# Cache pages with two consecutive tokens per partition, on even and odd partitions

## What is computed

```python
# sample attention: block-sparse (MoBA), blocks of 256 tokens = 2 pages, best 3 of 8 blocks
page_sum = jnp.sum(cache_k[layer_idx, page_table].astype(jnp.float32), axis=2)
...
kmean = jnp.sum(page_sum.reshape(bsz, nb, pages_per_block, N_HEADS, HEAD_DIM), axis=2) / MOBA_BLOCK
gate = jnp.einsum('bthd,bnhd->bthn', q, kmean)        # chooses the blocks
s = jnp.einsum('bthd,bthnd->bthn', q, k_g) / math.sqrt(HEAD_DIM)
s = s - slopes[None, None, :, None] * dist            # ALiBi: dist = position of q - position of key
p = jax.nn.softmax(jnp.where(valid, s, -jnp.inf), axis=-1)
att = jnp.einsum('bthn,bthnd->bthd', p, v_g)
...
z = x @ w_in                                          # [q | k | v | B | C | h], 1024 x 3072
mix = jnp.concatenate([att, gb * conv_y], axis=-1) @ w_out
x1 = layer_norm(DEEPNORM_ALPHA * x + mix, ln1_g, ln1_b)
up, ffn_buf_new = causal_dwconv(x1 @ w_up, ffn_buf, w_fconv)
f = (jax.nn.silu(a) * g) @ w_down                     # a, g = split(up)
y = layer_norm(DEEPNORM_ALPHA * x1 + f, ln2_g, ln2_b)
```

## Time and profile before

| | |
|---|---|
| three runs | 440.43, 440.23, 439.62 us |
| their median | 440.23 us |
| the profiled execution's own time | 439.81 us |
| span from its first to its last instruction | 438.0 us |
| PE, DVE, ACT, POOL busy | 412.9, 295.2, 181.2, 106.5 us |
| DMA packets, bytes | 109515, 124.86 MB |
| mean TensorE clock granted | 0.991 |

### The profile page before, as it was taken

The page is one execution under the profiler, slowest core; times in us unless marked ns, Lnnn a source line. Parts: engine busy times, 40 slices in busy tenths (PEclk is TensorE's granted clock), DMA queues, the critical chain, the costliest instruction groups (busy, mean ns, idle before and its releaser), DMA issues.

```text
span 438.0 us, 8235 instructions
## 1 busy us (share of the span) xinstructions
PE 412.9 (94%) x2903; PEld 339.1 (77%) x2903; DVE 295.2 (67%) x382; ACT 181.2 (41%) x694; POOL 106.5 (24%) x133
## 2 busy tenths in 40 slices
PE   5999999999999998999999989999999999999990
PEld 5588887876866774765554479999999999999990
DVE  0498999999799976954441274667766776534437
ACT  1587469644378233112110234544455555233201
POOL 1004134995255221100000707122211221000002
PEclk9999999999999999999999999999999999999996
DMA  8999999899999999999999933655566665667002
GB/s 316 393 362 407 405 407 378 323 393 408 410 353 364 354 400 405 405 405 404 404 402 402 353 113 97 193 172 160 162 179 194 196 194 179 190 202 215 2 1 99
DMA packets 109515, 124.86 MB, mean 285 GB/s; under 512 B 5775, under 2 KB 66920, under 8 KB 109466
## 3 DMA queue, kind: packets, MB, share of 16 engines
q1 hardware_dynamic: 101138, 107.56, 69.9%
q10 hardware_dynamic: 8336, 16.78, 10.2%
HBM read 121.90 MB, written 2.61 MB: 284 GB/s over the span
## 4 chain that ended last, share of the span: by engine, by line
PE 57%; DVE 18%; SPq 9%; issue 6%; DMA 5%; POOL 2%; ACT 1%; DVEq 0%; POOLq 0%; ACTq 0%
PE ps L1807 11%; PE ps L1808 11%; PE ps L1809 11%; SPq L352 7%; DVE qk L929 6%; DVE T L939 5%; PE ps L1700 4%; PE ps L1424 4%; PE ps L1619 4%; PE ps L1595 3%; PE ps L1621 3%; PE ps L1371 3%; DMA wring<-in_cache_v 2%; DMA KV<-in_cache_k 2%; POOL x1l L603 1%
## 5 line engine op out<-in xcount | busy, mean ns | idle before, releaser
L1176 DVE TENSOR_TENSOR wlo<-KV,whi 128x2048 fp32r<-128x2048 f32 (+1 forms) x24 | 61.8, 2575 | 57.1 <-ACT whi L829 29.1
L1424 PE MATMUL ps<-xT,wring 128*128 128x264 f32 x384 | 89.6, 388 | 0.1
L1424 PEld LDWEIGHTS ps<-xT,wring 128*128 128x128 f32 x384 | 71.6, 190 | 13.5 <-issue 1.7
L1807 PE MATMUL ps<-x1h,whi 128*128 128x264 f32 x256 | 73.7, 288 | 0.2
L1808 PE MATMUL ps<-x1l,whi 128*128 128x264 f32 x256 | 72.6, 284 | 0.0
L1809 PE MATMUL ps<-x1h,wlo 128*128 128x264 f32 x256 | 72.5, 283 | 0.0
L929 DVE TENSOR_TENSOR qk<-KV,qk 128x1536 f32<-128x1536 f32 (+1 forms) x32 | 67.5, 2111 | 5.7 <-DMA KV<-in_cache_k 2.2
L660 ACT ACTIVATE qk<-qk 128x64 f32<-128x64 f32 x216 | 51.8, 245 | 29.7 <-POOL qk L551 21.6
L939 DVE TENSOR_REDUCE T<-qk 128x24 f32<-128x1536 f32 (+1 forms) x32 | 58.4, 1827 | 0.0
L1807 PE MATMUL ps<-fh,whi 128*128 128x264 f32 x176 | 50.3, 286 | 0.1
L1808 PE MATMUL ps<-fl,whi 128*128 128x264 f32 x176 | 49.9, 284 | 0.0
(11 more groups left out here) (213 smaller groups left out, 572.4 us busy)
## 6 DMA issues: line engine op xcount, KB each, us to landing
KV<-in_cache_k SPq DMA_DIRECT2D x128, 256.0 KB, 6.5
KV<-in_w_ffn_up SPq DMA_DIRECT2D x32, 512.0 KB, 4.7
KV<-in_cache_v SPq DMA_DIRECT2D x60, 256.0 KB, 7.9
wring<-in_cache_v SPq DMA_DIRECT2D x56, 256.0 KB, 6.9
KV<-in_w_ffn_down SPq DMA_DIRECT2D x8, 1408.0 KB, 6.4
wring<-in_w_in ACTq DMA_DIRECT2D x5, 2048.0 KB, 14.1
zbuf<-in_cache_v SPq DMA_DIRECT2D x12, 256.0 KB, 5.2
zbuf<-in_w_ffn_up SPq DMA_DIRECT2D x3, 1024.0 KB, 10.3
```

What stands on the lines that cost most here:

```text
L1176: nc.vector.tensor_tensor(wlo[s][:, 0:n], w2[s][:, 0:n], whi[s][:, 0:n], ALU.subtract).then_inc(s_lo, 1)
L1424: ins = nc.tensor.matmul(ps[:, z_bank(n), 0:R], tile[k], xT[:, k, :], start=k == 0, stop=k == KT - 1)
L1807: nc.tensor.matmul(out, wh[k], xh[k], start=k == 0, stop=False)
```

## The change

`load` keeps its four `dma_start` for a group and their order, but each page now goes to every second partition. Page g of a group lands on the partitions of parity g % 2, and fills there the columns of both pages of its pair (g - g % 2 and the next): token 2i lies in the first of them, token 2i+1 in the second, on partition 2i + g % 2. In HBM the two tokens are 4 KB in a row, and in SBUF the two columns are 4 KB in a row. In the built program each of these DMAs has 64 rows of 1024 floats on either side (a step of two partitions on the SBUF side), where it had 128 rows of 512. There are 256 such DMAs, so their packets fall from 32768 to 16384; the bytes stay.

A block's 512 rows of K (or V) fill the same 128 x 2 places as before in another order, so nothing else changes but the table of distances. No instruction is added, removed or moved on any engine.

```diff
             def load(pages, ids, dst, landed):
                 for g in range(GP):
-                    sp.dma_start(dst[:, g, :], pages[bass.ds(ids[g], 1)].rearrange("o t d -> (o t) d")).then_inc(landed, 16)
+                    sp.dma_start(dst[g % 2:P:2, g - g % 2:g - g % 2 + 2, :],
+                                 pages[bass.ds(ids[g], 1)].rearrange("o (t j) d -> (o t) j d", j=2)).then_inc(landed, 16)
...
     tok = np.arange(P)
-    past = PAST - (np.arange(NPAGE)[None, :] * PAGE + tok[:, None])
+    g = np.arange(NPAGE)[None, :]
+    past = PAST - ((g - g % 2 + tok[:, None] % 2) * PAGE + tok[:, None] // 2 * 2 + g % 2)
```

## The result

The changed kernel takes 449.44 us (median of four runs, 447.76 to 451.94) where the kernel before takes 440.33 (four runs, 439.62 to 441.15). The ratio is 1.0212, with a 95% interval of 1.0171 to 1.0254: slower by 9.1 us. Forecast were 438.5 and a gain as the likeliest sign. The profiled execution took 448.5 us, with a span of 446.7; that of before had 439.81 and 438.0. In the changed kernel all lines behind L352 stand one higher, so L1596 is the `values` of before's L1595.

What follows compares the result with a forecast made beforehand. The V stretch was taken as bounded nearly equally by the page stream and PE's own list. Terms -1.7 + 1.9 - 1.9 = -1.7 gave 438.5 us against the median, own range 436.6 to 440.3, 8-in-10 range 436.6 to 452.

Steps and rivals of the forecast that it cites:

- What costs nothing: SP's page issues, the other engines' work and the clock: no cost; a 64-row issue, 0 to 0.5 us, stays under 0.62.
- rival 1: Page writes to SBUF: even and odd partitions collide, rate under 403 GB/s, price 455 us, ends 441 and 484; chance 0.30.
- Term 1: V stream, 150 to 240 us: 425 GB/s in place of 403 closes PE's gaps on DMA, -1.7 us.
- Term 2: K part: `w_in` gets less beside 4 KB pages, chunk 2 lands late, `z_tile(8)` stalls, +1.9 us (1.1 to 3.7).
- Rival 2: K part: K never runs dry, so `w_in` starves at several chunks, 442.3 us; chance 0.08.
- Term 3: PE's gaps at 67.57 (for ACT) and 100.68 us (for DVE's penalties) swallow the lateness from `z_tile(8)`, -1.9 us.
- Rival 3: Page stream: 4 KB pages run at 403 GB/s too, no faster rate, 440.2 us; chance 0.08.
- The clock: Whole kernel: granted clock was 1.00 in each window; with fewer gaps no cause was seen for another.

Runs made afterwards that it cites:

- spwait4: The kernel before with four already-true waits on SP behind each page load, taking only SP's time: 444.75 us, ratio 1.0109.
- fixed_after: The changed kernel with constant page numbers in place of the page table, so table reads and register instructions are gone: 440.81 us, ratio 1.0020 to the kernel before.
- filled: The changed kernel with four unread matmuls added on PE ahead of two waits in the V part: 448.63 us, ratio 1.0206 to the kernel before.
- pairs_k: The kernel before with the change's load for K pages alone, V pages loaded as before: 445.04 us, ratio 1.0114.
- fixed_before: The kernel before with constant page numbers, so table reads and register instructions are gone: 439.42 us, ratio 0.9981.
- pairs_v: The kernel before with the change's load for V pages alone, K pages loaded as before: 442.97 us, ratio 1.0062.
- spwait6: The kernel before with six already-true waits on SP behind each page load, taking only SP's time: 456.19 us, ratio 1.0329.

## Why the prediction was wrong, step by step

**The step that failed: "What costs nothing".** It bounded the issue of a 64-row load at 0 to 0.5 us and said that "either stays under 0.62". The bound on the issue was right, 0.475. The comparison was wrong: it set the issue alone against the engines' time for a page. Before's own trace had the rest. The issue is 0.33, but SP goes from group to group in 2.07 us, so 0.52 for a page; 0.18 of that are register instructions and the time between instructions. With them, the upper bound was 0.5 + 0.18 = 0.68, above 0.62, and the edit had a price. The page table's 0.97 us for each sample, 0.06 for a page, was left out as well. Measured are 0.67, or 0.73 with the table, against 0.63. `spwait4` shows that 0.12 us more for a page is enough for 4.6 us. A slow issue was no rival of mine with a chance. That 449.4 lies inside the range of 436.6 to 452 is luck: the range reached that far only for rival 1's cost.

**Term 1, -1.7 for the V stream.** The rate was there, a little under the 425 taken: 414 to 420 GB/s in full windows against 403 to 406. But the gain was not, nor in `fixed_after`, where SP is level with the engines: there PE still waits 1.9 us for V pages in total, against 1.7. I had treated PE's gaps as a want of rate. When pages start is set by homes that PE frees and by when SP comes to them, so at the places of the gaps 3% more rate changed little; with SP well ahead this is not tested. Over the change as made the term was a loss: 382 GB/s, 2.15 us more gaps and 3.4 us of half clock. Of the 408.7 GB/s of the Trainium skill's page "DMA: Bandwidth & Descriptors", section "iDMA fabric — 4 AXI ports for 8 engines, asymmetric across TPBs", the trace says what the window at 419 had said: where the engines had work queued, 4 KB rows ran at 414 (186 to 204 us, with two weight loads among them) and 418 (116 to 123, beside `w_out`) here.

**Term 2, +1.9 for `w_in`.** Right in kind and nearly in size. PE's gap ahead of `z_tile(8)`, in the changed kernel and in `fixed_after`:

```profile
52.31 3.80 PE L1425 MATMUL ps<-xT,wring 128*128 128x264 f32 x16 [1.14 <-issue]
```

```profile
52.44 3.80 PE L1426 MATMUL ps<-xT,wring 128*128 128x264 f32 x16 [1.61 <-issue]
```

The gap is put down to "issue", but before had none there. Chunk 2 landed 16.9 us after its issue at 35.3, so at 52.2, just ahead of `z_tile(8)`. The time is inside the 16 to 18 foretold and up from 14.8. It goes with the form of the K pages: 16.9, 17.1, 17.4 and 17.8 us in the change, `filled`, `fixed_after` and `pairs_k`, but 14.7 and 14.8 in `fixed_before` and `pairs_v`, which have no such wait. The waits are 1.1, 1.3, 1.6 and 2.0 us. That the slower SP makes it milder, since K then takes fewer turns, would fit the first three but not `pairs_k`, whose SP is as slow there. The other side agrees: `wo_mix`, whose packets stay at 4 KB while those of the pages beside it double, lands after 13.3 us and not 11.4. So turns by packets hold, near the low end of the term. The prediction's sentence that gets the third from the Trainium skill's page "DMA: Bandwidth & Descriptors", section "Queues, rings and completion order", goes further than the page: its packet is a run of typically 9 to 17 descriptors, not one row, so the third stands on the rows and landings here alone. Rival 2, a starving at several chunks, did not come: no other chunk has a wait of that kind in any of these traces.

**Term 3, -1.9 from gaps that absorb it.** Half right at best. In `fixed_after` the gap at 67 us is gone, but it is gone in `pairs_v` too, where `z_tile(8)` had not waited, so one trace does not show that lateness closed it. The one ahead of the penalties stays: 0.86 before, 0.87 in the change, 0.85 in both fixed kernels, though the penalties begin anywhere from 100.7 to 103.4 in them. I had said that it goes at DVE's pace; it moves with PE, which fits penalties that follow PE's own sums. So of 1.9 only 1.0 could be had. In the change not even that: the wait for ACT behind z tiles is 1.96 (at 70.25) and not 1.01; in `filled`, the same program there, it is 1.01.

**What the sum would have been.** With the layout and SP level with the engines, terms 0 + 1.6 - 1.0 give +0.6 by the parts of `fixed_after`; measured are 0.6 against before and 1.4 against `fixed_before`. With SP's time per page the loss follows, but its size does not: gaps of one or two microseconds and the clock behind them are not read from a rate.

**Rival 1** covered the amount (its ends were 441 and 484, its price 455) by a wrong mechanism: even and odd partitions do not collide (415 GB/s); halves do. **Rival 3**, no faster rate, is refuted by the windows. The clock, for which I had seen "no cause", fell as well, each time right behind a wait of 2.37 or 1.97 us that the late pages and weights made.

**What stays open.** Why 64 rows or a step lengthen the issue; why an issue takes longer with a constant page number; what the faster rate is worth to a kernel whose SP is ahead; whether K and V in the new form cost more together than apart; how much of the total is the clock's over many runs; and why the runs of the change scatter by 4 us. Whether a cheap form of 4 KB packets exists was not found: the cheap form with larger packets, 32 neighbouring rows of 8 KB, puts a page on a quarter of the partitions, and halves were already at 307 GB/s. No kernel here computes the same and beats the one before.

## What to carry to other kernels

When a transfer's shape changes, work out the issuing queue's whole time for one transfer, from start to start in its timeline, with register instructions and table reads, and hold it against the engines' time for the same bytes; here 0.58 against 0.65 us was a lead, and 0.73 against 0.63 cost 2% of the whole time. The issue's own row is not enough: with constant page numbers it went from 475 to 597 ns while SP's time from start to start fell from 0.67 to 0.64 us. A faster rate is worth only the waits that a slow rate makes; here the waits hardly moved with it, perhaps since PE itself frees the homes that the pages need. To tell a slow queue from slow memory, look at rate, DMA share and the time from issue to landing (344 GB/s at 0.97 with 4.3 us was a late issuer, 307 at 1.04 was busy engines on half of the partitions), and slow the issuer alone in the old kernel as a test.

## What the hardware showed that I had not expected

- The issue of a load on SP's queue depends on the rows and their step, not on bytes: 333 ns for 128 rows (of 1 KB or 2 KB), 317 for 96, 316 for 32 or 16, but 469 for 64, 513 for 64 from partition 32 on, 466 to 475 with a step of 2 or 4, and 537 to 543 for 64 rows in two pieces each. All this with the page number in a register; with a constant in its place, 432 for 128 rows and 597 for 64 with a step of 2.
- 64 neighbouring partitions at a time ran at 307 GB/s, every second partition at 414 to 418 where work was queued, with the same packets.
- Packets of 4 KB in place of 2 KB raise the full rate by some 3% (415 over 404), and take turns from a queue with smaller packets: its 2 MB took 16.9 to 17.8 us in place of 14.7 to 14.8.
- Behind the waits of 2.37 and 1.97 us in the V part the granted clock stood at half for 3.4 us each; behind one of 1.96 us at 70.25 in the same execution it did not fall. Of the other traces, `spwait4` has such a stretch from the end of a wait of 3.02 us and `spwait6` behind waits of 3.12, 2.35 and 2.27, and `pairs_k` has none behind one of 2.01.
